# In the attention steps, ScalarE's exponentials ahead of the filling stage's work, and branch A's merge stages by halves

## The reference

```
h = layer_norm(x) * (1 + scale) + shift
qa, ka, va, ga, qb, kb, vb, gb, uc, vc, gc = split(h @ w_in)
a_out = softmax(qa ka^T, latent keys and cached context keys) va     # 8 query heads, 2 key heads
b_out = softmax(qb kb^T, window of 128, context keys, sink) vb
c_out = uc * (w_spatial mixed over chunks of layer_norm(vc))
ya = (a_out * silu(ga)) @ w_proj_a ; yb, yc likewise
g_a, g_b, g_c = sigmoid(h @ w_gate + b_gate)
y  = (g_a * ya + g_b * yb + g_c * yc) @ w_out
x  = layer_norm(alpha * x + gate * y)
```

## Time and profile before

| | us |
|---|---|
| median of 3 runs | 1380.17 |
| lowest and highest | 1379.47, 1381.62 |
| profiled execution | 1381.45 |
| its span | 1379.6 |
| TensorE busy in it | 1350.9 (98%) |
| VectorE, ScalarE, GpSimd busy | 770.1, 630.2, 682.8 |

### The profile page before, as it was taken

One profiled execution on the slowest core, in us unless ns is written; L12 is line 12 of the kernel. 1 busy time (PEld: TensorE's weight loads), 2 busy tenths in 40 slices (PEclk: granted clock), 3 DMA queues, 4 the chain that ended last, 5 costly groups with the idle time before them and its releaser, 6 DMA issues.

```text
span 1379.6 us, 22530 instructions
## 1 busy us (share of the span) xinstructions
PE 1350.9 (98%) x8646; PEld 1256.8 (91%) x8646; DVE 770.1 (56%) x1634; ACT 630.2 (46%) x1330; POOL 682.8 (49%) x490
## 2 busy tenths in 40 slices
PE   7999999999999999999999999999999999999997
PEld 5898999899899999999888989998989989999986
DVE  5756773263883511655685577732468725036558
ACT  5446886244764221213264478843367733222130
POOL 3456565334665344344653666643356544445450
PEclk9999999999999999999999999999999999999999
DMA  9312001221013254354321220012120042125321
GB/s 376 131 62 81 16 31 47 77 81 62 32 47 123 76 174 151 104 209 134 132 105 42 74 76 31 32 47 80 62 77 31 32 138 77 61 77 199 126 88 77
DMA packets 36762, 126.88 MB, mean 92 GB/s; under 512 B 5040, under 2 KB 5808, under 8 KB 36656
## 3 DMA queue, kind: packets, MB, share of 16 engines
q1 hardware_dynamic: 29952, 108.54, 23.0%
q10 hardware_dynamic: 6704, 16.90, 3.4%
HBM read 119.66 MB, written 5.77 MB: 91 GB/s over the span
## 4 chain that ended last, share of the span: by engine, by line
PE 82%; DVE 4%; POOL 2%; ACT 2%; issue 1%; DVEq 0%; ACTq 0%; POOLq 0%
PE ps L996 30%; PE ps L981 17%; PE ps L925 6%; PE ps L927 6%; PE ps L926 6%; PE ps L1146 4%; PE ps L1159 2%; PE ps L1160 2%; PE ps L1136 2%; PE ps L1138 2%; POOL w_lo L1870 1%; DVE top L1721 1%; PE ps L1167 1%; PE ps L1013 1%; PE ps L1029 1%
## 5 line engine op out<-in xcount | busy, mean ns | idle before, releaser
L1870 POOL TENSOR_TENSOR w_lo<-raw,w_hi 128x1024 fp32r<-128x1024 f32 x148 | 360.1, 2440 | 269.3 <-ACT w_hi L1203 206.7
L1203 ACT ACTIVATE w_hi<-raw 128x1024 fp32r<-128x1024 f32 x148 | 154.1, 1054 | 151.4 <-DMA raw<-in_weights 65.9
L996 PE MATMUL ps<-h_hi,w_hi 128*128 128x320 f32 x736 | 170.2, 313 | 0.0
L981 PE MATMUL ps<-h_hi,w_hi 128*128 128x320 f32 x544 | 168.8, 310 | 0.2 <-DVE q_t L1690 0.2
L981 PE MATMUL ps<-h_hi,w_lo 128*128 128x320 f32 x544 | 168.2, 309 | 0.0
L981 PE MATMUL ps<-h_lo,w_hi 128*128 128x320 f32 x544 | 168.0, 309 | 0.0
L996 PE MATMUL ps<-h_hi,w_lo 128*128 128x320 f32 x736 | 168.0, 309 | 0.0
L996 PE MATMUL ps<-h_lo,w_hi 128*128 128x320 f32 x736 | 167.5, 309 | 0.0
L996 PEld LDWEIGHTS ps<-h_hi,w_hi 128*128 128x128 f32 x736 | 127.0, 189 | 11.2 <-issue 1.6
L925 PE MATMUL ps<-w_hi,h_hi 128*128 128x512 f32 (+1 forms) x360 | 129.2, 359 | 1.2 <-POOL w_lo L1870 1.0
L927 PE MATMUL ps<-w_hi,h_lo 128*128 128x512 f32 (+1 forms) x360 | 127.6, 354 | 0.0
(11 more groups left out here) (201 smaller groups left out, 3120.5 us busy)
## 6 DMA issues: line engine op xcount, KB each, us to landing
raw<-in_weights SPq DMA_DIRECT2D x190, 512.0 KB, 3.3
raw_more<-in_weights SPq DMA_DIRECT2D x10, 512.0 KB, 10.1
x<-in_x_sample ACTq DMA_DIRECT2D x6, 512.0 KB, 9.6
x_mid<-x ACTq DMA_DIRECT2D x5, 512.0 KB, 2.6
x<-x_mid ACTq DMA_DIRECT2D x5, 512.0 KB, 6.2
y_sample<-x SPq DMA_DIRECT2D x3, 512.0 KB, 2.6
pack<-in_pack ACTq DMA_DIRECT2D x2, 528.0 KB, 6.2
x<-in_x_sample SPq DMA_DIRECT2D x2, 512.0 KB, 5.1
```

Source lines behind the costliest of these rows:

```text
L981: last = pe.matmul(ps[:, s, 0:HALF], w[:, u % RING, first + k * P:first + (k + 1) * P], acts[:, k, half * HALF:(half + 1) * HALF], start=o ...
L996: last = pe.matmul(ps[:, s + half, 0:HALF], w[:, u % RING, cols], acts[:, k, half * HALF:(half + 1) * HALF], start=k == 0 and part == 0, s ...
L1203: did(act.activation(w_hi[:, n % RING, :], raw_tile(r), ACT.Copy), hi_made)
L1870: did(pool.tensor_tensor(w_lo[:, n % RING, :], raw_tile(r), w_hi[:, n % RING, :], ALU.subtract), w_ready)
```

## The change

Three edits, all in the planner but for the copies that follow from them.

In `attention`, the exponentials of a step are put ahead of the filler's chunks and events of that step. TensorE's order is not touched by this, since the exponential is no event of TensorE's; ScalarE's is. A split that stands behind the filler's chunk is now behind the exponentials too.

All `z` stages of branch A (r = 0) are made by halves, the ones with j > 0 in banks 6 and 7. The first half's event stands behind the fourth of the stage's 8 chunks. The copy into `merge` is made for each half, and `sg`, the sigmoid later on, waits for both halves of every j.

```diff
 def by_halves(stage):
-    return stage[0] == "gT" or stage[0] == "y" and stage[2] == 0 or stage[0] == "z" and stage[2:] == (0, 0)
+    return stage[0] == "gT" or stage[0] in ("y", "z") and stage[2] == 0

 def in_steps(stage):
+    if stage[0] == "z":
+        return stage[2] == 0 and stage[3] > 0
     return stage[0] == "gT" and (stage[2] in ("c", "u") or stage[2:] == ("b", KT_B - 1))
@@ attention
         if n >= lag:
             product(n - lag)
+        out.extend(exps[n])
         fill()
-        out.extend(exps[n])
@@ layer_order
         filler.extend(chunks(("z", l, 0, j), 8))
+        filler[-5] = (filler[-5], first_half(("z", l, 0, j)))
         filler[-1] = (filler[-1], ("z", l, 0, j))
@@ ScalarE
-                    elif kind in ("z1", "z") and e[2:] == (0, 0):
+                    elif kind in ("z1", "z") and e[2] == 0:
                         s, first = wait_filled(act, e), HALF * (kind == "z")
-                        did(act.activation(merge[:, 0, first:first + HALF], ps[:, s, 0:HALF], ACT.Copy), drained[s])
+                        did(act.activation(merge[:, e[3], first:first + HALF], ps[:, s, 0:HALF], ACT.Copy), drained[s])
@@
-                        if j == 0:
-                            wait_drained(act, ("z1", l, 0, 0))
+                        wait_drained(act, ("z1", l, 0, j))
                         wait_drained(act, ("z", l, 0, j))
```

More of the change, by code:

```diff
@@ L1417, in _ @@
                         s = wait_filled(act, e)
[L1418 to L1421, removed]
+                        if r > 0:
                             n = 2 * KT_D * l + (r - 1) * KT_D + j
```

## The result

The changed kernel takes 1384.94 us (median of 6 runs, 1384.89 to 1386.15), the kernel before on the same chip 1381.47 us (1379.47 to 1382.58). The ratio is 1.0029 with a 95% interval of 1.0018 to 1.0040: **slower by 0.29%**. The forecast was 1382.5 us, "no difference to be seen" as the likeliest and slower next to it. The time lies in the range, 2.4 us over the forecast: 1.3 us because the kernel before came out that much higher than the 1380.17 us from which the forecast counted, and 1.2 us in the sum (+3.5 in place of +2.3 us). It just misses "no difference to be seen".

The account below looks back on a forecast made before the run. TensorE was taken as the bound, busy 1350.9 of 1379.6 us, with about 4 us of waits removable. Terms 0.91 + 0.74 - 0.4 + 1.06 = +2.3 us against the 1380.17 us median gave 1382.5 us, range 1378.5 to 1385.5.

Parts of the forecast that it names:

- no difference to be seen: Whole kernel: time within 0.2% (2.8 us) of the kernel before; chance 0.52.
- A, step 0, layer 0: Branch A's first attention step: split behind the exponential delays p_hi and the transpose waiting for GpSimd, +0.91 us, bounds 0 to 1.05.
- A, step 0, layer 1: Same step in layer 1: split behind the exponential delays the first P·V product, +0.74 us, bounds 0 to 1.05.
- Nothing is added: Branch A, layer 1: normalisations end at 819.25, before the transpose of 819.7 wants them, so no further loss.
- A, later steps: Branch A after step 0, both layers: merge copies by halves behind the exponentials remove waits, -0.4 us in all.
- B, step 2: Branch B, each layer: score product gains 0.46 us, late tanh and w_lo delay the next transpose; net +0.53 us a layer.
- (a): Rival: waits for exponentials go, late tanh and splits are absorbed; 1376.4 us, chance 0.12.
- (b): Rival: reordering reaches only 12 of 72 steps a layer, only the 0.4 us is left; 1379.8 us, chance 0.12.
- (c): Rival: new waits lower TensorE's clock after 130 us; 1384.2 us for one fall, 1387.6 with both branches B; chance 0.16.

Follow-up runs that it names:

- mended order: Changed kernel with `cv` ahead of the steps, A's split before the exponential, B's before gate copy and tanh, gate multiplication ending step 5: 1379.60 us, ratio 0.9986.

## Why the forecast was right, and where not

**A, step 0, layer 0: +0.91 forecast, +1.81 measured at that transpose.** This step failed, by a hold that the sum had at nothing. ScalarE's part was right (p_hi late by 0.94; T of step 3 late by 0.50 against 0.55). I carried p_hi's lateness along VectorE with the durations of the trace before, `cv` among them at 0.62 us. But w_lo follows w_hi on another engine; I carried that in B and forgot it in A. Carried, it begins at 133.5 (measured 133.49), and `cv`, which ends 0.15 us behind it, holds the sum until 135.94. The chain by p_hi that the forecast did carry was priced right: with `cv` away in both kernels it costs 0.96 us, against 0.91. The bound that I set at the top, 1.05 ("the whole split"), was therefore no bound: the split moved by 2.06 us, from 130.31 to 132.37, not by its length. And the 0.62 us for an operation whose siblings of the same size take 0.28 was a sign in the trace of before.

**A, step 0, layer 1: +0.74 forecast, +0.69 measured**, by the chain that was named. "Nothing is added" at the transpose behind it was off by 0.12, by `cv` again: it goes with `cv` moved away.

**A, later steps: -0.4 forecast, -0.5 measured**, a quarter of a microsecond in each layer. The -0.15 is the halves' part: it is missing where the exponentials alone are moved. The -0.10 comes with either edit alone.

**B, step 2: +0.53 a layer forecast, +0.53 and +0.52 measured.** Each stage of the chain was where it was put: -0.44 against -0.46, w_lo 0.74 us later and the normalisations 1.4 us later than before in the same frame, the wait of 0.35 us behind it covered. What the working blended together, the runs took apart: 0.61 us of VectorE behind tanh and 0.71 us of GpSimd behind w_lo. Undoing the first alone left the second; the second was not undone alone.

**Not in the sum at all: +0.14 at 719 us and +0.28 in B's step 14 of layer 1.** The first comes and goes between executions, whatever the edit. The second is in every trace that has the halves and in no other. There ScalarE starts the sink's exponential 0.38 us behind the maximum instead of 0.10, with ScalarE idle in the profile for that long. Why was not tried and stays open.

**The rivals.** (a), the waits simply go: the -0.44 us a layer in B is real, and a mended order keeps it, but the rest is given back at once. (b), too few steps to matter: the steps with waits are the ones that were hit. (c), the clock: no stretch below full speed after 130 us in the changed kernel, up to TensorE's last matmul. It is no empty rival, though. In the kernel with `cv` on w_lo, where TensorE idled 1.37 us ahead of T of step 3 at 135.65, the clock fell soon after; the window from 137 us:

```profile
137.00:142.00 5.00, 5.00 (x23) 4.58 (x23) 2.98 (x8) 2.65 (x7) 2.75 (x3) 0.66 0.02 5
```

A wait alone doesn't bring it down: in the same trace the first P·V of layer 1 idled 2.33 us at 817.27, and the clock of 815 to 825 us was 1.00.

The sum came to +3.5 us in place of +2.3, of which 0.90 is the one term of A's layer 0 and 0.42 the two unforeseen places (0.14 of them a matter of the execution).

**The range held the time in part by luck.** Its upper end of 1385.5 us was set by one fall of the clock, and none came. Without it the bounds of the terms reach 1380.17 + 1.05 + 1.05 - 0.4 + 1.8 = 1383.7 us, and the 1384.94 us lie above that: the term of A's layer 0 broke its bound by 0.76 us, and the kernel before came out 1.3 us higher. The lower end, by the same bounds, is 1378.9 us and not 1378.5.

## What to carry to other kernels

When an operation is moved behind another on its engine, its new start is set by the end of what it now stands behind, not by its own length; carry every engine that follows it, one list at a time. A short operation that takes twice as long as its siblings in one place is held by something there, and may be held for longer if that something moves. What a reordering gives at the wait it aims at is kept only if the operations tied to the same spot (here a split and a multiplication) are placed anew as well.

## What the runs showed of the hardware

VectorE's operation with both inputs in SBUF is held until GpSimd's operation beside it ends: the low part of 128x128 took 0.28 us alone, and 0.62, 1.48 and 2.47 us as more of a w_lo of 2.4 us lay ahead of it, ending 0.15 us behind it; the gate multiplication of 0.82 us took 2.37 us and ended 0.68 us behind it. The profile shows no wait for this: the held operation starts at its place, and its duration grows. It goes both ways: a normalisation of GpSimd took 1.62 us instead of 1.04 behind such an operation of VectorE.

TensorE's granted clock was at its lower level for one stretch near 117 us in ten of thirteen traces and at full in three, of nearly the same kernel. Two of these three have no fall of the clock at all before TensorE's last matmul and are 1.6 and 2.0 us ahead of the kernel before at 122 us (0.15 and 0.47 us of that at 20 us already). A difference under 3 us in this kernel needs many runs, or the starts of the same matmuls compared.
